# The last up projection of a four-block transformer kernel: 36 of its 44 tiles in pairs, by seven products of half size

## The reference, cut to what matters

```python
def swiglu(h, w_gate_up, w_down):
    g, u = jnp.split(h @ w_gate_up, 2, axis=-1)      # 1024 -> 2 x 2816
    return (jax.nn.silu(g) * u) @ w_down             # 2816 -> 1024
...
h = modulate(rms_norm_2(x, norm_gains[i, 2]), sh_f, sc_f)
h = swiglu(h, w_gate_up[i], w_down[i])
x = x + g_f[:, None, :] * rms_norm_2(h, norm_gains[i, 3])
```

## Time and profile before

| | us |
|---|---|
| three runs, lowest, median, highest | 2111.04, 2113.28, 2115.69 |
| the profiled execution | 2112.06 |
| its span, first to last instruction | 2110.3 |
| TensorE busy in it | 2065.2 |
| VectorE busy | 1286.4 |
| ScalarE busy | 864.8 |
| GpSimd busy | 143.3 |
| mean granted TensorE clock | 0.995 |

### The profile page before, as it was taken

The page is one execution under the profiler, slowest core; times in us unless marked ns, Lnnn a source line. Parts: engine busy times, 40 slices in busy tenths (PEclk is TensorE's granted clock), DMA queues, the critical chain, the costliest instruction groups (busy, mean ns, idle before and its releaser), DMA issues.

```text
span 2110.3 us, 29091 instructions
## 1 busy us (share of the span) xinstructions
PE 2065.2 (98%) x11424; PEld 1710.7 (81%) x11424; DVE 1286.4 (61%) x2287; ACT 864.8 (41%) x1547; POOL 143.3 (7%) x155
## 2 busy tenths in 40 slices
PE   8999999999999999998899999999999999999998
PEld 6877779888888988786779888888988898888887
DVE  5378747877765688538955877755556464333324
ACT  4267754544431354439734534331332243222221
POOL 0000002000000200005502000000110020000001
PEclk9999999999999999999999999999999999999999
DMA  8110002323256333335332332346322223333331
GB/s 275 61 41 21 22 11 91 110 92 98 88 174 217 101 93 100 100 111 168 114 101 70 110 100 91 93 154 238 104 84 96 77 74 101 100 90 97 90 91 63
DMA packets 69688, 216.93 MB, mean 103 GB/s; under 512 B 8112, under 2 KB 11568, under 8 KB 69296
## 3 DMA queue, kind: packets, MB, share of 16 engines
q1 hardware_dynamic: 67536, 208.72, 31.2%
q10 hardware_dynamic: 2016, 6.36, 0.9%
HBM read 211.70 MB, written 2.23 MB: 101 GB/s over the span
## 4 chain that ended last, share of the span: by engine, by line
PE 48%; DVE 2%; ACT 2%; POOL 1%; issue 0%; ACTq 0%; DVEq 0%
PE bank L815 16%; PE bank L817 15%; PE bank L819 15%; POOL h L710 1%; PE bank L760 1%; ACT ebuf L1664 0%; ACT sqr L1664 0%; PE bank L791 0%; DVE zb L2449 0%; DVE ylo L2434 0%; PE bank L1244 0%; PE bank L807 0%; DVE wlo L1850 0%; PE bank L1269 0%; PE bank L1247 0%
## 5 line engine op out<-in xcount | busy, mean ns | idle before, releaser
L815 PE MATMUL bank<-xhi,whi 128*128 128x512 f32 (+1 forms) x1832 | 701.1, 383 | 14.7 <-DVE xlo L1864 7.8
L817 PE MATMUL bank<-xlo,whi 128*128 128x512 f32 (+1 forms) x1832 | 693.1, 378 | 0.0
L819 PE MATMUL bank<-xhi,wlo 128*128 128x512 f32 (+1 forms) x1832 | 693.0, 378 | 0.0
L1374 ACT ACTIVATE whi<-raw 128x1024 fp32r<-128x1024 f32 (+1 forms) x319 | 331.0, 1040 | 706.9 <-PE bank L819 680.3
L1850 DVE TENSOR_TENSOR wlo<-raw,whi 128x1024 fp32r<-128x1024 f32 (+1 forms) x319 | 385.6, 1210 | 288.6 <-ACT whi L1374 288.3
L815 PEld LDWEIGHTS bank<-xhi,whi 128*128 128x128 f32 x1832 | 345.7, 189 | 90.1 <-issue 12.8
L819 PEld LDWEIGHTS bank<-xhi,wlo 128*128 128x128 f32 x1832 | 345.6, 189 | 69.2
L817 PEld LDWEIGHTS bank<-xlo,whi 128*128 128x128 f32 x1832 | 346.0, 189 | 66.7
L815 PE MATMUL bank<-hid_hi,whi 128*128 128x512 f32 (+1 forms) x624 | 226.4, 363 | 0.0
L819 PE MATMUL bank<-hid_hi,wlo 128*128 128x512 f32 (+1 forms) x624 | 224.8, 360 | 0.0
L817 PE MATMUL bank<-hid_lo,whi 128*128 128x512 f32 (+1 forms) x624 | 224.7, 360 | 0.0
(11 more groups left out here) (284 smaller groups left out, 2420.2 us busy)
## 6 DMA issues: line engine op xcount, KB each, us to landing
raw<-w SPq DMA_DIRECT2D x295, 512.0 KB, 3.6
ada_w<-w_ada SPq DMA_DIRECT2D x64, 384.0 KB, 4.1
raw<-w SPq DMA_DIRECT2D x24, 384.0 KB, 3.3
row<-cum_rows SPq DMA_DIRECT2D x32, 256.0 KB, 3.5
xbuf<-exp_rows SPq DMA_DIRECT2D x24, 256.0 KB, 3.6
w_k<-w_cmp ACTq DMA_DIRECT2D x1, 2048.0 KB, 10.8
w_v<-w_cmp ACTq DMA_DIRECT2D x1, 2048.0 KB, 8.6
out_t<-h SPq DMA_DIRECT2D x16, 128.0 KB, 1.7
```

The source lines that it names most:

```text
L815: pe.matmul(bk[:, tok], whi[w][:, cols], hi[:, k, tok], start=k == 0, stop=False, skip_group_check=split)
L817: pe.matmul(bk[:, tok], whi[w][:, cols], lo[:, k, tok], start=False, stop=False, skip_group_check=split)
L819: return pe.matmul(bk[:, tok], wlo[w][:, cols], hi[:, k, tok], start=False, stop=last, skip_group_check=split)
L1374: act.activation(whi[g % SLOTS][:, 0:n], raw[g % RAWS][:, 0:n], ACT.Copy).then_inc(s_hi, 1)
```

## The change

The first eight tiles of `UP3` (`CLASSIC`) stay as they are. The other 36 become 18 pairs of a gate panel and a value panel. A pair is a matrix of 2 x 2 blocks: A11 and A12 are the gate panel's halves over the input features (512 each), A21 and A22 the value panel's. The operand is split in the same way into input halves and token halves (HEAD, TAIL). In place of eight products of a half panel (4 blocks) with 256 tokens there are seven, `P1` to `P7`, in Winograd's form. Each is 4 blocks by 3, that is 12 matmuls of 128 x 256.

- **Operand sums.** Four sums of operand quarters (`t_f`, then `t_hi` and `t_lo`, 128 x 1024 each) are made once, during the first tiles of `UP3`: `operand_sum` and `sums_lo` on DVE, `sums_hi` on ACT. The seam's scaled values are kept in `mt` for that, in place of the two-buffer `tmp`.
- **Weight sums.** Four sums of half panels for each pair are made by GpSimd (`wsum`, L877, L879, L882, L884 of the new kernel), 128 x 512 each, 72 in all.
- **Units.** The high and low parts are made in five units for each pair: A11, A12 and A22 of 512 columns, S21 (two sums) and S34 (two sums) of 1024. A pair had two units of 1024 before.
- **Products.** TensorE goes P1, P6, P5, P7, P2, P4, P3, into three banks X, Y, Z: P1 and P2 into X, P6, P7 and P4 into Y, P5 and P3 into Z. Each bank accumulates over its products. In between, ACT copies P1 out (`first_p`), and DVE makes five sums of 256 columns (`part`, each a bank plus an SBUF tile). Part 1 must be done before P7, part 2 before P4, part 3 before P3.
- **Hidden tiles.** The product with the silu (`pair_hidden`, L2880) now reads two SBUF tiles. The hidden tiles' high parts go to the room of the operands as these come free: 4 of them during the pairs 1 to 4, the other 18 during the last pair and the first tile of `DOWN3`. `DOWN3` reads them there; for some blocks the 512 columns are two pieces of 256.
- **Others.** A fourth `raw` buffer serves the pairs. The signal copies on DVE give way to plain semaphore increments.

```diff
+CLASSIC = 8
+PAIR0 = START["UP3"] + CLASSIC
+PAIRS = (TILES["UP3"] - CLASSIC) // 2
+ORDER_P = ("P1", "P6", "P5", "P7", "P2", "P4", "P3")
+UNIT_PLACE = {"A11": (0, 0, 4), "S21": (1, 0, 8), "A12": (0, 4, 4), "S34": (2, 0, 8), "A22": (3, 0, 4)}
+UNIT_LAST = {"A11": "P1", "S21": "P5", "A12": "P2", "S34": "P3", "A22": "P4"}
...
+                pool.tensor_tensor(s1, a21, a22, ALU.add).then_inc(s_wsum, 1)
+                pool.wait_ge(s_wsum, 4 * n + 1)
+                pool.tensor_tensor(s2, s1, a11, ALU.subtract).then_inc(s_wsum, 1)
+                if n:
+                    pool.wait_ge(s_ulo, unit_made(n - 1, "S34"))
+                pool.tensor_tensor(s3, a11, a21, ALU.subtract).then_inc(s_wsum, 1)
+                pool.wait_ge(s_wsum, 4 * n + 2)
+                pool.tensor_tensor(s4, a12, s2, ALU.subtract).then_inc(s_wsum, 1)
...
+                    pair_product(n, "P5", "Z")
+                    pe.wait_ge(s_part, 5 * n + 1)
+                    pair_product(n, "P7", "Y")
+                    pe.wait_ge(s_p1, n + 1)
+                    pair_product(n, "P2", "X")
+                    pe.wait_ge(s_part, 5 * n + 2)
+                    pair_product(n, "P4", "Y")
+                    pe.wait_ge(s_part, 5 * n + 3)
+                    pair_product(n, "P3", "Z")
...
+            for n in range(PAIRS):
+                unit_hi(n, "S34")
+                if n:
+                    pair_silu(n - 1, TAIL)
+                act.wait_ge(s_prod, product_done(n, "P1"))
...
+                act.activation(first_p[:, n % 2, :], half_of(pair_bank(n, "X")), ACT.Copy).then_inc(s_p1, 1)
+                unit_hi(n, "A22")
+                unit_hi(n + 1, "A11")
+                unit_hi(n + 1, "S21")
+                if 1 <= n < 5:
+                    hidden_hi(n - 1)
...
+                unit_hi(n + 1, "A12")
+                pair_silu(n, HEAD)
...
+            for n in range(PAIRS):
+                if n:
+                    part(n - 1, 5, c12[:, :], "Z", "P3", part_u[:, 0, :])
+                unit_lo(n, "S34")
+                if n:
+                    pair_hidden(n - 1)
+                dve.wait_ge(s_p1, n + 1)
+                part(n, 1, part_u[:, 0, :], "Y", "P6", first_p[:, n % 2, :])
+                unit_lo(n, "A22")
+                unit_lo(n + 1, "A11")
+                if 1 <= n < 5:
+                    hidden_lo(n - 1)
+                part(n, 2, part_u[:, 1, :], "Y", "P7", first_p[:, n % 2, :])
...
+                part(n, 3, rise[:, cols_of(TAIL)], "Z", "P5", part_u[:, 1, :])
+                unit_lo(n + 1, "S21")
+                unit_lo(n + 1, "A12")
...
+                part(n, 4, rise[:, cols_of(HEAD)], "Y", "P4", first_p[:, n % 2, :])
```

More of the change, by code:

```diff
@@ L386, in build @@
         stat_ps, bc_ps = bank[5], bank[4]
[L388 removed]
+        s_raw = [sem(f"raw_landed{k}") for k in range(RAWS + 1)]
         s_x = [sem(f"x_tile_landed{k}") for k in range(KD)]
@@ L814, in product @@
                 cols = slice(kb * P, (kb + 1) * P)
[L815 to L820, removed]
+                x_hi = hi(k, tok) if callable(hi) else hi[:, k, tok]
@@ L858, in project_in @@
                     lead(TAIL, (3,))
-                for t in range(first, TILES[name]):
+                for t in range(first, CLASSIC if name == "UP3" else TILES[name]):
                     for (tile, _), extra in between:
@@ new lines, in sums_lo, with unit_lo @@
+            def sums_lo(t):
+                dve.wait_ge(s_thi, t + 1)
+                dve.tensor_tensor(t_lo[:, t, :, :], t_f[:, t, :, :], t_hi[:, t, :, :].bitcast(F32), ALU.subtract)\
+                    .then_inc(s_tlo, 1)
+            def unit_lo(n, unit):
+                if n >= PAIRS:
+                    return
+                place, k0, nb = UNIT_PLACE[unit]
+                w, cols = slot_of(place), slice(k0 * P, (k0 + nb) * P)
+                if unit in ("S21", "S34"):
+                    src = wsum[:, (0 if unit == "S21" else 2):(2 if unit == "S21" else 4), :]\
+                        .rearrange("p a n -> p (a n)")
+                else:
+                    g = PAIR0 + 2 * n + (unit == "A22")
+                    src = raw[RAW_OF[g]][:, 0:S] if unit == "A11" else raw[RAW_OF[g]][:, S:2 * S]
+                dve.wait_ge(s_uhi, unit_made(n, unit))
+                dve.tensor_tensor(wlo[w][:, cols], src, whi[w][:, cols].bitcast(F32), ALU.subtract)\
+                    .then_inc(s_ulo, 1)
@@ L2580, in _ @@
-            low3(21)
-            project_out("DOWN3", m_x, Q_F3_POST)
+                    dve.tensor_tensor(hid_f[c // 2][:, :], in_bank(c)[:, :], silu_, ALU.mult).then_inc(s_hid, 1)
+                    dve.wait_ge(s_hid, MADE["UP3"] + 2 * KD + c // 2 + 1)
+                    dve.sem_inc(s_ev, 1)
+                if c < CLASSIC - SLOTS:
+                    weight_lo(st + c + SLOTS)
+                    if c < 3:
+                        operand_sum(c + 1)
+                elif c == CLASSIC - SLOTS:
+                    sums_lo(0)
+                    sums_lo(1)
+                    unit_lo(0, "A11")
+                elif c == CLASSIC - SLOTS + 1:
+                    sums_lo(2)
+                    sums_lo(3)
+                    unit_lo(0, "S21")
+                    unit_lo(0, "A12")
@@ new lines, in _ @@
+            hidden_lo(7)
+            hidden_lo(8)
+            part(PAIRS - 1, 5, c12[:, :], "Z", "P3", part_u[:, 0, :])
+            weight_lo(START["DOWN3"] + 1)
+            hidden_lo(9)
+            hidden_lo(10)
+            pair_hidden(PAIRS - 1)
+            for k in range(11, KF):
+                hidden_lo(k)
+                if k == 13:
+                    weight_lo(START["DOWN3"] + 2)
+                if k == 17:
+                    weight_lo(START["DOWN3"] + 3)
+            project_out("DOWN3", m_last, Q_F3_POST)
```

328 lines of the change are left out of this document (272 added, 56 removed).

## The result

| | before | after |
|---|---|---|
| median us (lowest to highest) | 2113.40 (2111.04 to 2115.69), 4 runs | 2098.78 (2095.53 to 2104.00), 4 runs |
| profiled execution, span | 2112.06, 2110.3 | 2104.00, 2102.3 |
| start of the seam's first residual update on GpSimd | 1707.44 | 1715.96 |
| from there to the end of the span | 402.9 | 386.3 |

The kernel became faster: the ratio is 0.9921, with a 95% interval of 0.9908 to 0.9935. In times that is 14 to 19 us; the forecast was 17.2 us less and 2096.0, with a range of 2090 to 2105.

The account below looks back on a forecast made before the run. TensorE's matmul stream was taken to bound the kernel. Terms -22.1 + 2.6 + 2.0 + 0.3 = -17.2 us, from 2113.28 to 2096.1, stated as 2096; range 2090 to 2105.

Parts of the forecast that it names:

- What bounds the kernel: In nearly all of `UP3`, time is TensorE's matmuls alone: busy 228.00 of 228.00 us.
- The matmuls, -22.1: In the 18 pairs, 84 matmuls of 256 columns replace 48 of 512: 201.6 to 179.5 us if TensorE never waits.
- P4 in the pairs 1 to 4, +2.6: Where a `hidden_lo` precedes part 2, P4 starts about 0.65 us late in each of four pairs.
- P4 in the 13 others, +2.0: Part 2 ready with nothing to spare; P4 taken as 0.15 us late in each pair without `hidden_lo`.
- The hold: 1.13 or 1.27: A GpSimd sum holds VectorE up 1.13 us by the trace; the skill's wording means 1.27, ending at 2099.
- Into `DOWN3`, +0.3: Late conversion of 18 hidden tiles during `DOWN3`'s first tile costs 0.3 us, between 0 and 3.
- Tiles 0 to 7, the seam, SP: Operand sums in `UP3`'s first tiles, the seam's lost buffer wait and SP's panel issues: nothing; tiles at worst 5 us once.
- a pair over 10.6 us: Sign in the new profile that would prove the forecast wrong; about 10.1 us between P1s was expected.
- a wait before P7: Sign against the forecast: no wait before P7 was expected, with part 1 having 0.5 us to spare.
- The clock: Rival: brief product waits in the pairs lower TensorE's clock, making the kernel slower, 2115 us and more; 2%.

Follow-up runs that it names:

- Experiment 5: The kernel before, with tiles 8 to 43 of `UP3` multiplied in token halves (128 x 256 matmuls): median 2119.46 us, ratio 1.0013 to before.
- experiment 3: The changed kernel with GpSimd's weight sums 16 columns wide in place of 512, except in pair 0: median 2094.72 us, ratio 0.9900 to before.
- experiment 1: The changed kernel run again, unaltered: median 2097.88 us, ratio 0.9918 to before, 385.9 us from the seam.
- experiment 2: The changed kernel with part 2 ahead of A11's low part and `hidden_lo` in VectorE's queue: median 2096.15 us, ratio 0.9905 to before.
- experiment 6: The changed kernel with GpSimd making each pair's third weight sum twice, five sums a pair: median 2109.03 us, ratio 0.9965 to before.

## Why the prediction was right, point by point

- **What bounds the kernel.** TensorE's stream, to 98.8% of the pairs even now. Right.
- **The matmuls, -22.1.** Experiment 5 gives -22.2. In experiment 3, which has the order of after without its holds, the pairs take 180.4 us, of which 0.9 is what all its steps have beyond 0.1187: 179.5, or -22.1. Right within 0.1.
- **P4 in the pairs 1 to 4, +2.6.** Start to start 0.45, 0.58, 0.66 and 1.05, and a slow second step (0.1) in each: 3.1. Without the late panel in the fourth it would be some 2.7. By the whole pairs, P7's wait among them, it is 3.6 more than 4 x 9.97, or 2.9 without the late panel. Right.
- **P4 in the 13 others, +2.0.** 10.14 - 9.97 = 0.17 us each, and 10.01 in the last: 2.1. Right, though I had said "the lateness hangs on 0.1 us in each of six terms". It held because the terms did. Counted from a P1 at 1854.97 (P4's start less 7.12), the forecast and the rows are: S34 low done 2.7 and 2.7, part 1 done 3.7 and 3.6, A11 low done 6.7 and 6.7, part 2 done 7.1 and 7.0, S21 low done 8.7 and 8.6, A12 low done 9.3 and 9.2.
- **The hold: 1.13 or 1.27.** The rows are met by 1.13, to 0.04 us. The Trainium skill, "SBUF — State Buffer", "Who interferes with whom", has the lock last for the whole instruction, and the result would then have been 2099. (The section also names more cases of the lock than the "two SBUF inputs only" of the prediction.) That 2099 lies near the median is no point for it: P4 is 0.4 late in none of the 13 pairs.
- **Into `DOWN3`, +0.3.** No wait for the late hidden tiles; the first steps of 512 columns are 0.30 and 0.23 us long. 0.1 at most. The forecast's margin of "nothing to spare" for k = 18 to 21 was too pessimistic, but it was only +0.3.
- **Tiles 0 to 7, the seam, SP.** All put at nothing. From the seam's start to the first matmul of the pairs it is 65.2 us, where it was 65.4, and from `DOWN3`'s first matmul to the end 136.0, where it was 135.9. Right. In the pairs it is -22.1 + 5.6 = -16.5, with 5.6 for what all steps in the pairs have beyond 0.1187; the forecast had 4.6 for it.
- **Missed.** Two of the signs that were to prove the forecast wrong came: "a pair over 10.6 us" in pairs 2, 3 and 4 (10.72, 10.74, 11.45), and a wait before P7 in pair 4. The first was set too close, as the forecast itself gave 9.97 + 0.65 = 10.62 for these pairs. Behind the second, and behind the 11.45, stands what the prediction does not have, a panel that lands late. Before, one late panel cost nothing: ScalarE's one wait of 0.7 us for a panel lies in a stretch in which TensorE is never idle. In the pairs it moves GpSimd's sums on to other low parts. It cost 0.7 us in after, 0.9 in experiment 1 and, twice in one execution, more than 1 in experiment 2.
- **The clock.** 1.00 in the pairs of every kernel here, also in experiment 6 with TensorE idle 8.6 of 193 us. The rule of the Trainium skill that was a rival ("TensorE: Matmul & The Clock Gate", "A second HAM failure mode: psum-queue depth-cycling") did not show itself: waits of 0.3 to 1.7 us between groups, with three banks in turn, left the clock alone.

The median came 2.8 us above the forecast. Of that, the profile accounts for some 0.6 (16.6 in place of 17.2 us from the seam); the rest is inside what repeats of one kernel differ by. In the second comparison the ratio puts the kernel 17 us below before; that this is so near the 17.2 of the forecast is luck.

The experiments give two versions that are as good or better. With part 2 earlier, or with the sums on VectorE, the stretch from the seam is 4.0 to 4.8 us shorter than in after, and the medians are 1.7 and 3.2 us lower. The intervals of the ratios overlap with that of after, so only the profiles separate them.

## What to carry to other kernels

When work is given to an idle engine that takes turns with a busy one at its operands, as GpSimd does with VectorE here, count what it takes from the busy one: here 1.13 us of VectorE for a sum that VectorE does in 0.69. Then look in the busy engine's queue for the one result that another engine waits for, and place it so that no operation that can be held up stands ahead of it; but a place so early that the queue must wait for its input is only free while the time is lost anyway. And compare two kernels over the stretch that the change touches, since what lies ahead of it can differ by more than the change from one execution to the next.

## What the hardware showed that I had not expected

- An operation of VectorE that reads a bank is not slowed at all beside GpSimd (413 ns on average in after, 424 with narrow sums), and one with two SBUF inputs takes whole holds, not a share: 0.69 becomes 1.44 or 1.78, depending on when the sum ahead began.
- Doing the four sums on VectorE left VectorE's busy time where it was: 1392.8 against 1389.3 us.
- A GpSimd sum of 16 columns still takes 0.22 us (experiment 3), and 0.57 to 0.74 when it comes first after a wait, so the time of a small GpSimd operation is mostly not its columns.
- One panel or two in an execution take 5.0 us to land where the median is 3.3, with the DMA share at 0.30. All 15 panels over 4.0 us in seven profiles met a 16 KB packet of the queue `instruction`; that this is the cause is argued from the traces and not tested.
